# Pairs of weight chunks split by one instruction in the first layer's experts, and the router in column tiles

## The reference

```python
x = x + ga1 * out_l
h2_l = modulate(rmsnorm(x, g_norm2[i]), sh2, sc2)      # rmsnorm * (1 + scale) + shift
aff = sigmoid(h @ w_router); sel = aff + b_router      # 16 scores per token
# group of 4 experts by its best two; the two best experts in it; gates from aff
for e in range(16):
    he = silu(h @ w_e_gate[e]) * (h @ w_e_up[e])
    y = y + gates[:, e:e+1] * (he @ w_e_down[e])
```

## Time and profile before

| | us |
|---|---|
| median of three runs | 1566.52 |
| lowest, highest | 1563.4, 1567.39 |
| the profiled execution | 1565.73 |
| its span, first to last instruction | 1563.8 |

### The profile page before, as it was taken

How to read it: one execution, slowest core, us unless ns; L and a number is a source line. 1 busy time by engine, 2 the same in 40 slices (tenths; PEclk the granted TensorE clock), 3 DMA queues, 4 the chain that set the end, 5 groups by cost and what they waited for, 6 DMA issues and landing times.

```text
span 1563.8 us, 20838 instructions
## 1 busy us (share of the span) xinstructions
PE 1393.5 (89%) x7774; PEld 1019.3 (65%) x7774; DVE 791.1 (51%) x1268; ACT 674.7 (43%) x1098; POOL 166.8 (11%) x194
## 2 busy tenths in 40 slices
PE   5699999999998987999999955999989877998882
PEld 2478777885557855788888844998875865543330
DVE  1512344425775536999999937474358642000002
ACT  3442122334664224788888844542257530111002
POOL 4210110002320001021111120000000001111001
PEclk9699999999998996999999987999999987999997
DMA  8663564325862223899999962463230458999994
GB/s 297 240 221 131 189 242 148 95 95 189 257 201 95 95 81 119 304 380 383 383 380 376 365 230 87 143 221 108 95 135 1 149 202 321 414 416 415 414 415 160
DMA packets 117078, 359.35 MB, mean 230 GB/s; under 512 B 14570, under 2 KB 14891, under 8 KB 116355
## 3 DMA queue, kind: packets, MB, share of 16 engines
q1 hardware_dynamic: 91410, 272.86, 47.6%
q0 software_dynamic: 24720, 82.21, 15.0%
q10 hardware_dynamic: 864, 3.15, 0.5%
HBM read 345.57 MB, written 25.17 MB: 237 GB/s over the span
## 4 chain that ended last, share of the span: by engine, by line
PE 76%; DMA 13%; DVE 5%; ACT 3%; issue 2%; POOL 1%; POOLq 0%; SPq 0%; ACTq 0%; DVEq 0%
PE ps L545 18%; PE ps L547 18%; PE ps L546 18%; DMA ring<-in_w_e_gate 9%; PE ps L1085 3%; PE ps L797 3%; PE ps L911 2%; PE ps L888 2%; PE ps L815 2%; DMA w_raw<-in_w_ada 1%; PE ps L1107 1%; DMA ring<-in_w_e_down 1%; PE ps L1028 1%; PE ps L981 1%; PE ps L899 1%
## 5 line engine op out<-in xcount | busy, mean ns | idle before, releaser
L541 DVE TENSOR_TENSOR w_lo<-w_raw,w_hi 128x1024 fp32r<-128x1024 f32 x224 | 270.9, 1224 | 309.3 <-ACT w_hi L537 307.4
L537 ACT ACTIVATE w_hi<-w_raw 128x1024 fp32r<-128x1024 f32 x224 | 235.5, 1058 | 326.4 <-PE ps L547 324.5
L545 PE MATMUL ps<-h_hi,w_hi 128*128 128x512 f32 (+1 forms) x704 | 249.5, 354 | 14.8 <-DVE h_lo L1527 9.1
L546 PE MATMUL ps<-h_lo,w_hi 128*128 128x512 f32 (+1 forms) x704 | 246.9, 351 | 0.0
L547 PE MATMUL ps<-h_hi,w_lo 128*128 128x512 f32 (+1 forms) x704 | 246.9, 351 | 0.0
L545 PEld LDWEIGHTS ps<-h_hi,w_hi 128*128 128x128 f32 x704 | 133.9, 190 | 37.0 <-DVE h_lo L1527 9.9
L1085 PE MATMUL ps<-ring,xT 128*64 128x256 f32 x1024 | 131.2, 391 | 17.8 <-DMA ring<-in_w_e_up 10.8
L546 PEld LDWEIGHTS ps<-h_lo,w_hi 128*128 128x128 f32 x704 | 134.0, 190 | 18.6 <-issue 0.2
L547 PEld LDWEIGHTS ps<-h_hi,w_lo 128*128 128x128 f32 x704 | 133.9, 190 | 18.7
L1085 PEld LDWEIGHTS ps<-ring,xT 128*64 128x64 f32 x1024 | 68.8, 138 | 80.9 <-DMA ring<-in_w_e_up 25.7
L541 DVE TENSOR_TENSOR w_lo_more<-w_raw,w_hi_more 128x1024 fp32r<-128x1024 f32 x96 | 115.3, 1223 | 5.2
(11 more groups left out here) (258 smaller groups left out, 2366.0 us busy)
## 6 DMA issues: line engine op xcount, KB each, us to landing
w_raw<-in_w_ada POOLq DMA_DIRECT2D x96, 512.0 KB, 5.5
w_raw<-in_w_e_gate SPq DMA_DIRECT2D x64, 512.0 KB
w_raw<-in_w_e_up SPq DMA_DIRECT2D x64, 512.0 KB
w_raw<-in_w_e_down SPq DMA_DIRECT2D x64, 512.0 KB
ring<-in_w_e_gate SPq DMA_DIRECT2D x64, 512.0 KB, 15.6
ring<-in_w_e_up SPq DMA_DIRECT2D x64, 512.0 KB
ring<-in_w_e_down SPq DMA_DIRECT2D x64, 512.0 KB, 15.5
w_raw<-in_w_in SPq DMA_DIRECT2D x56, 512.0 KB
```

The source lines that it names most:

```text
L537: act.activation(whi(n), raw[:, slot(n), :, :], ACT.Copy).then_inc(hi_ready, 1)
L541: dve.tensor_tensor(wlo(n), raw[:, slot(n), :, :], whi(n).bitcast(F32), ALU.subtract).then_inc(lo_ready, 1)
L545: pe.matmul(acc, sh, mh, start=first, stop=False, skip_group_check=True)
L546: pe.matmul(acc, sh, ml, start=False, stop=False, skip_group_check=True)
```

## The change

1. In the first layer's experts `split_hi2` and `split_lo2` handle two neighbouring chunks in one instruction of 128x2048. Each waits for both transfers and for the later of the two ring places, and signals both when done. The small steps that stood after three of four chunks now stand after two.
2. The router no longer reads `h2T`. Scores are computed from `X` itself: weights `wrs` = router x scale, made once by DVE, times `X`; the shift's part is a sum of its own, 16 matmuls with one column (8 in the second layer). `token_sums` puts this and the sums of squares into four tiles of 32 columns of the TensorE array. DVE copies the 128x257 result, three transposes turn it token-major, and the root, reciprocal and multiplication are done on small tiles (`token_scores`). The reciprocals are spread back to 128x512 by four transposes and a copy. `xn` has four buffers.
3. The tokens are turned in order of halves, behind `route`'s inputs.
4. In the first layer only the first group's `pick` and `ids` stay ahead of the experts; the other three are done among the first two experts' work (`later_picks`, `later_ids` on DVE and TensorE, in PSUM bank 7). POOL waits for the last of them before its first store.

```diff
+            for t in tiles[i]:
                 add_tile((i, "h2", t, half), "act")
         add_tile((i, "rank"), "dve")
-        for g in range(4):
...
+    def hi_lo(n):
+        r, hi_, lo_ = n % (2 * SPL), (whi4, whi8), (wlo4, wlo8)
+        two = slice(r % SPL, r % SPL + 2)
+        return hi_[r // SPL][:, two, :, :], lo_[r // SPL][:, two, :, :]
+
+    def split_hi2(act, n, it=None, per=0):
+
+        for m in (n, n + 1):
+            act.wait_ge(raw_in[slot(m)], raw_value(m, it, per))
+        act.wait_ge(w_used, scaled(n + 1 - 2 * SPL + 1, it, per))
+        act.activation(hi_lo(n)[0], raw[:, slot(n):slot(n) + 2, :, :], ACT.Copy).then_inc(hi_ready, 2)
+
+    def split_lo2(dve, n, it=None, per=0):
+        dve.wait_ge(hi_ready, scaled(n + 2, it, per))
+        hi_, lo_ = hi_lo(n)
+        dve.tensor_tensor(lo_, raw[:, slot(n):slot(n) + 2, :, :], hi_.bitcast(F32), ALU.subtract).then_inc(lo_ready, 2)
...
-                wait_emptied(pool, (i, "ids", 3))
+                pool.wait_ge(ids_out, 3)
...
+        def token_sums(i, ks):
+
+            key, o = (i, "n2"), KT * norms[f"n2_{i}"]
+            acc = bank(key)
+            sides = [(0, 1), (1, 0)][i:]
+            if ks[0] == 0:
+                take_tile(pe, key)
+                pe.wait_ge(small_in, 32)
+                pe.wait_ge(mod_b, i + 1)
+                for k in range(KT):
+                    for g, st in sides:
+                        r0 = 64 + 32 * g
+                        pe.matmul(acc[r0:r0 + NE, SEQ:SEQ + 1], wr[:, k, :], mod[i][:, 24 + k, st:st + 1],
+                                  start=k == 0, stop=k == KT - 1, skip_group_check=True)
+            for k in ks:
+                pe.wait_ge(n_sq, o + k + 1)
+                for g, st in sides:
+                    tc = slice(g * SEQ, (g + 1) * SEQ)
+                    pe.matmul(acc[32 * g:32 * g + 32, 0:SEQ], ones[:, 0:32], sq[:, k % 2, tc],
+                              start=k == 0, stop=k == KT - 1, skip_group_check=True)
+                    r0 = 64 + 32 * g
+                    m = pe.matmul(acc[r0:r0 + NE, 0:SEQ], wrs[:, k, st, :], X[:, k, tc],
+                                  start=False, stop=k == KT - 1, skip_group_check=True)
                 m.then_inc(n_squ if k < KT - 1 else tile_done, 1)
...
-            norm_sum(f"n2_{i}", (i, "n2"), c0, range(4, KT))
-            pe.wait_ge(small_in, 32)
-            key = (i, "log")
+            token_sums(i, range(4, KT))
+            wait_emptied(pe, (i, "n2"))
+            key = (i, "tk")
             take_tile(pe, key)
-            for k in range(KT):
-                pe.wait_ge(n_hf, KT * (2 * i + 1) + k + 1)
-                m = pe.matmul(bank(key)[0:NE, c0:T], wr[:, k, :], h2T[:, k, c0:T], start=k == 0, stop=k == KT - 1)
+            for j, src in enumerate((sums[:, 0:P], sums[:, P:2 * P], spread(sums[:, SEQ:SEQ + 1], [P, P]))):
+                m = pe.transpose(bank(key)[:, j * P:(j + 1) * P], src, ident)
...
-            key = (i, "aff")
+            key = (i, "rb")
             take_tile(pe, key)
             for t in tiles[i]:
-                m = pe.transpose(bank(key)[:, NE * t:NE * t + NE], affT[0:NE, t * P:(t + 1) * P], ident[0:NE, 0:NE])
+                m = pe.transpose(bank(key)[:, t * P:(t + 1) * P], spread(rstd[:, t:t + 1], [P, P]), ident)
...
+            def turn_h2(half):
+                pe.wait_ge(n_hf, KT * norms[f"n2_{i}"] + 4 * half + 4)
+                for t in tiles[i]:
...
+            turn_h2(0)
+            turn_h2(1)
...
+            def later_ids(g):
+                if g >= 2:
+                    pe.wait_ge(ids_out, g - 1)
+                slot_ids(g, ps[:, 7, :]).then_inc(ids_done, 1)
...
                     into_hidden(nb + 8 * e, e, 0)
+                    later_ids(1 + 2 * e)
                     if e:
                         turn_hidden(0)
                     into_hidden(nb + 8 * e + 4, e, 1)
+                    if e == 0:
+                        later_ids(2)
...
-            norm_rms(f"n2_{i}", col0[i])
-            act.wait_ge(mod_b, 1)
+            t0, key = tiles[i][0], (i, "tk")
+            wait_tile(act, key)
+            act.activation(std4[:, t0:].rearrange("p (g j) -> p g j", j=2),
+                           bank(key)[:, 0:2 * P].rearrange("p (j g c) -> p g j c", j=2, c=32)[:, i:2, :, 0],
+                           ACT.Sqrt, bias=epst[:, 0:1], scale=1.0 / D).then_inc(n_std, 1)
+            warm(ACT.Sigmoid)
+            wait_emptied(act, key)
+            act.activation(aff[:, t0:, :], lg[:, t0:, :], ACT.Sigmoid).then_inc(aff_ready, 1)
+            act.wait_ge(mod_b, i + 1)
             norm_apply(f"n2_{i}", col0[i], lambda k, s: sc2[i][:, k, s:s + 1], lambda k, s: mod[i][:, 24 + k, s:s + 1], False)
...
-            key = (i, "log")
-            warm(ACT.Sigmoid)
-            wait_tile(act, key)
-            act.activation(affT[0:NE, col0[i]:T], bank(key)[0:NE, col0[i]:T], ACT.Sigmoid).then_inc(free_act, 1)
-            for t in tiles[i]:
-                for half in range(2):
+            for half in range(2):
...
-                    split_hi(act, n + ch, it, 24)
+                for ch in range(0, count, 2):
+                    split_hi2(act, n + ch, it, 24)
...
-                        splits(n + 8, 3, it)
+                        splits(n + 8, 2, it)
                         result(n + 4, 2 * it + j, j, it)
-                        splits(n + 11, 1, it)
...
+                    xn_, room = (xn[:, k % 2], 2) if split else (xn4[:, k % 4], 4)
+                    if k >= room:
+                        dve.wait_ge(n_hf, o + k - room + 1)
+                    dve.tensor_tensor(xn_[:, c0:T], X[:, k, c0:T], rinv[:, c0:T], ALU.mult).then_inc(n_xn, 1)
...
+                    dve.wait_ge(small_in, 32)
+                    for st in range(2):
+                        ins = dve.tensor_tensor(wrs[:, :, st, :], wr[:, :, :], spread(sc2[i][:, :, st:st + 1], [P, KT, NE]), ALU.mult)
+                    link(ins)
...
+            t0, c0 = tiles[i][0], col0[i]
+            key = (i, "n2")
+            wait_tile(dve, key)
+            dve.tensor_copy(sums[:, :], bank(key)[:, 0:SEQ + 1]).then_inc(free_dve, 1)
+            key = (i, "tk")
+            turned_ = bank(key)[:, 0:3 * P].rearrange("p (j g c) -> p g j c", j=3, c=32)[:, 2 + i:4, :, 0:NE]
+            by_tile = lambda t_: t_.rearrange("p (g j) e -> p g j e", j=2)
+            dve.wait_ge(n_std, i + 1)
+            link(dve.reciprocal(rstd[:, t0:], std4[:, t0:]))
+            link(dve.tensor_tensor(by_tile(lg[:, t0:, :]), turned_[:, :, 0:2, :],
+                                   by_tile(spread(rstd[:, t0:].unsqueeze(2), [P, 4 - t0, NE])), ALU.mult))
+            dve.tensor_tensor(by_tile(lg[:, t0:, :]), by_tile(lg[:, t0:, :]),
+                              spread(turned_[:, :, 2:3, :], [P, 2 - i, 2, NE]), ALU.add).then_inc(free_dve, 1)
+            key = (i, "rb")
+            wait_tile(dve, key)
+            dve.tensor_copy(rinv[:, c0:T], bank(key)[:, c0:T]).then_inc(free_dve, 1)
...
+            picks(0)
+            if i == 0:
+                slot_ids(0)
+                for ch in range(0, 4, 2):
+                    split_lo2(dve, exp0[i] + ch)
+                return
+            for g in range(4):
+                if g < 3:
+                    picks(g + 1)
+                slot_ids(g)
+
+        def later_picks(g):
+            iota = spread(cs(C_IOTA, P).unsqueeze(1).unsqueeze(1), [P, 4, 4, P])
+            ex = slice(4 * g, 4 * g + 4)
+            dve.tensor_tensor(pick[:, :, ex, :], spread(mrank[:, :, ex].unsqueeze(3), [P, 4, 4, P]), iota,
+                              ALU.is_equal).then_inc(picked, 1)
+
+        def later_ids(g):
+            dve.wait_ge(ids_done, g)
+            dve.tensor_scalar(ids[:, 4 * g:4 * g + 4], ps[:, 7, 0:8:2], float(FAR), None, ALU.add).then_inc(ids_out, 1)
...
+                splits(nb + 4, 2)
+                later_picks(1)
+                splits(nb + 6, 2)
                 places(i)
-                splits(nb + 7, 1)
+                later_ids(1)
+                later_picks(2)
                 splits(nb + 8, 4)
+                later_ids(2)
                 tokens_lo(1)
+                later_picks(3)
                 hidden(nb + 8, 0)
-                splits(nb + 12, 4)
+                splits(nb + 12, 2)
+                later_ids(3)
+                splits(nb + 14, 2)
...
-                        splits(n + 8, 3, it)
+                        splits(n + 8, 2, it)
                         result(n + 4, 2 * it + j, j, it)
-                        splits(n + 11, 1, it)
+                        splits(n + 10, 2, it)
```

More of the change, by code:

```diff
@@ L232, in build @@
     wr = small("wr", [P, KT, NE])
+    wrs = small("wrs", [P, KT, 2, NE])
+    std4 = small("std4", [P, 4])
+    rstd = small("rstd", [P, 4])
     brb = small("brb", [P, NE])
@@ L444, in build @@
                 add_tile((i, "yT", k), "dve")
-    finish = {key: plan[(key[0], "WO", 1, 3)] + 0.5 if key[1:] == ("n2",) else t for key, t in plan.items()}
```

(32 more changed lines are left out.)

62 lines of the change are left out of this document (28 added, 34 removed).

## The result

The changed kernel takes 1578.36 us (median of 8 runs, 1572.53 to 1579.65) against 1566.98 (8 runs, 1563.4 to 1569.13): a ratio of 1.0066, 95% interval 1.0049 to 1.0083. It is 11.4 us slower. The forecast was 1558.3 us, with a range up to 1566; the case that came is the rival to which the prediction gave 1 in 10, the pairs that starve the DMA engines.

What follows compares the result with a forecast made beforehand. TensorE was taken to bound the first layer's experts, DVE and DMA close behind, with the router path exposed between projection and experts. Terms -7.0 - 4.7 + 6.5 + 0.7 - 3.7 = -8.2 us gave 1558.3 from 1566.5, range 1553.5 to 1566.

Steps and rivals of the forecast that it cites:

- the pairs that starve the DMA engines: First layer's experts: later, doubled loads run queues dry, 1.0 us an expert, +14, 1572 us; chance 0.10.
- Part 4, the pairs: First layer's steady stage: splitting chunks in pairs costs 0.05 us an expert for 14 experts, 0.7 us later.
- The slots' own loop is load, ACT, DVE: Steady stage: reloading a weight slot takes 10.1 us against 12.0 in which TensorE uses eight chunks, so it fits.
- 3.9 spare: Steady stage: TensorE needs a pair 8.4 us later, splits end at 4.5, leaving 3.9 us of slack.
- Part 1, sums on the way: First layer's projection: shift matmuls and packed sums make the last sum end net 0.6 us later.
- the rival of nearly free columns: Router's one-column matmuls in both layers cost almost nothing: 3.9 us less, 1554.4 us; chance 0.18.
- the packed row: adaLN product's profile row, eight 32-column records in 0.64 us, used to price one-column records at 0.08 us each.
- The column tiles do run together: Router sums: a tile's eight records take 0.64 us; the rival said 1.7, some 7 us in all, 1565, chance 0.04.
- Part 2: First layer, from last sum to `sel`: the new router path brings `sel` 7.0 us earlier, 8.7 after the last sum.
- Part 3, groups moved: First layer's first experts: moving three groups of `ids` gains 4.7 us before the transposes and costs 6.5 later.
- the prediction's other bound: First layer's first gather: with the second layer's gather time of 7.37 us, moving groups gains only 2.4 us.
- Part 5: Second layer's router: one-column matmuls add 1.3 us, the shorter path brings `sel` 3.7 us earlier.

Runs made afterwards that it cites:

- e1: The changed kernel with every chunk of the first layer's experts split singly on ACT and DVE, router and moved groups kept; 1558.44 us, 0.9948 of before.
- e3: The changed kernel with pairs on ACT alone, DVE splitting chunk by chunk; 1567.87 us, 1.0011 of before.
- e4: The changed kernel with pairs on DVE alone, ACT splitting chunk by chunk; 1565.93 us, 0.9991 of before.
- e8: The changed kernel with single splits and all four groups of ids ahead of the experts again, leaving only the router; 1554.62 us, 0.9928 of before.
- e10: The same kernel as e8, measured again; 1557.94 us, 0.9942 of before.
- e11: The same kernel as e1, measured again; 1559.45 us, 0.9956 of before.
- e5: The changed kernel with `xg_hi`, the hidden product and `xg_lo` ahead of the second gate pair; 1572.07 us, 1.0023 of before.
- e6: The changed kernel with only the gate pair directly ahead of `xg_hi` and `xg_lo` split in singles; 1568.62 us, 1.0006 of before.
- e7: The changed kernel loading only half of each down-weight chunk in the steady loop, a sixth fewer bytes, for timing only; 1568.72 us, 1.0004 of before.
- e9: The change made in e5, with `he_hi` and `he_lo` also moved ahead of a pair; 1573.61 us, 1.0032 of before.
- e13: The kernel of e9 with down-weight loads in the steady loop cut to half, a sixth fewer bytes; 1559.88 us, one run.
- e2: The kernel before with pairs alone on both engines, router and groups as before; 1581.6 us, 1.0097 of before.

## Why the prediction was wrong

*What bounds the kernel.* Right: TensorE bound the stage, DVE and the DMA engines (99.4%) close behind. The prediction saw how little was spare and then priced an edit that takes from it at 0.7 us.

*Part 4, the pairs: the step that failed.* 0.05 us an expert were taken; e1 against the change shows 1.2, 16.7 us in all and 20 in the medians. Two sentences carried it. "The slots' own loop is load, ACT, DVE", 10.1 "against the 12.0 us": it took 5.5 us for a load, from a stage where DMA had idle time. Here the gate loads in the chain took 6.5 to 7.9, and DVE's list adds the small steps and other pairs to the loop; it came to 18.5 to 19.9 for twelve chunks, against 18.0 that TensorE needs. "3.9 spare", for TensorE's need of a pair, counted weights only. `xg_lo` stands in the same list with 2.2 to spare, and the prediction did not look at it. The rival had the mechanism and nearly the size: with a loaded transfer of 7.4 it gave 12.65 for eight chunks, 1.0 an expert, 1572; the period of 19.16 is 12.8 for eight. What it lacked is the small steps behind the pair. It was held unlikely since "ACT waits for TensorE, not for transfers, so some slack is there". That wait was 0.3 us long each time, and the edit put 2.0 to 3.4 us into the loop: the slack should have been set against that number.

*Part 1, sums on the way.* That the total agrees (+0.8 for +0.6) is luck, and its terms are not right. Of the 32 one-column records 26 took 0.48 us together, 0.018 each, not 0.08; the rival of nearly free columns was true. The Trainium skill ("TensorEngine Tiling (Array Packing)", Instruction Overhead) leads to an estimated 0.025 a record, which the trace bears out better than the packed row did. That makes it 2.0 us cheaper than priced, so that the last sum should end 1.4 earlier than before, not 0.6 later. Over all profiled executions it does end earlier: at 578.5 on average in the sixteen kernels with the new router, at 579.4 and 579.9 in the two with the old one. With a scatter of 5.6 us that is a hint and no more. The column tiles do run together: the eight records of a tile stood within 0.64 us (577.53 to 578.17), as forecast.

*Part 2.* `sel` comes 9.07 us after the last sum, 8.7 were forecast; in every run with the router 9.05 to 9.54.

*Part 3, groups moved.* The price held: 1.84 us a group on TensorE (1.75 forecast), the second expert's products 24.2 us after the first transposes in e1 and 25.0 in the change (24.4 forecast), and 6.85 in all with single splits (6.5). The gain was 2.3 in place of 4.7 since the gather took 7.6 us from its issue to the first transposes; the prediction's other bound, 7.37 and a gain of 2.4, is what came. With single splits it takes 5.5 and the gain is 4.4: the missing 2.1 are the pairs' too, DVE's alone, as e3 and e4 show below.

*Part 5.* `sel` 5.99 after the last sum instead of 10.76: -4.8, forecast -5.0.

Without the pairs the sum would have been -8.9; e1 measured 8.3 under before, with a trace 5.6 shorter (its profiled execution was its slowest). For the router alone it would have been -10.7; e8 and e10 measured 12.2 and 9.8 under before, with traces 13.5 and 10.5 shorter.

## What to carry to other kernels

Before making an instruction longer in a pipeline that has room for N pieces, write the loop of one slot out in full, load, each engine and everything that stands between in its list, with load times from the same stage under the same traffic, and set it against the time in which the consumer uses N pieces. Then do the same for the small steps that stand behind the longer instruction: their slack, here 2.2 us, is not that of the weights. Here the DMA engines were over 99% full and the engine that the coarser pass relieved was not the bound: what it saved was worth nothing, and four more slots gave back, in the steady stage, the whole 1.2 us an expert that it cost.

## What the runs showed of the hardware

GpSimd's issue of the first gather takes longer beside a longer pass of DVE. The passes, the issue and the transposes that wait for the gather, in e3 (DVE in single splits, the first from 601.21 to 602.43):

```profile
601.21 4.62 DVE L545 TENSOR_TENSOR w_lo<-w_raw,w_hi 128x1024 fp32r<-128x1024 f32 x4
...
602.20 1.17 POOL L714 DMA_INDIRECT xg<-hbuf,ids  x1 [131.46 <-DVE ids L1805]
...
607.58 1.95 PE L1085 MATMUL ps<-cst,xg 128*128 128x128 f32 x8 [6.49 <-DMA xg<-hbuf,ids]
```

And in e4 (DVE in pairs, ACT in singles; the first pair from 602.43 to 604.72):

```profile
602.43 4.49 DVE L562 TENSOR_TENSOR w_lo<-w_raw,w_hi 128x2048 fp32r<-128x2048 f32 x2
...
603.42 2.25 POOL L714 DMA_INDIRECT xg<-hbuf,ids  x1 [133.14 <-DVE ids L1805]
...
611.13 1.95 PE L1085 MATMUL ps<-cst,xg 128*128 128x128 f32 x8 [8.82 <-DMA xg<-hbuf,ids]
```

1.17 against 2.25 us of issue, 5.4 against 7.7 us to the transposes. In both the issue ends 0.94 to 0.95 us after the pass beside which it started. The kernels with three groups moved fall into these two classes by DVE's splits alone: 5.4 to 5.5 in e1, e3 and e11, 7.6 to 7.7 in the change, e4, e5, e6, e7, e9 and e13. The Trainium skill ("SBUF — State Buffer", SBUF: two separate sides) says that a DVE instruction with two inputs in SBUF holds a port pair that it shares with GpSimd, for its whole length, against a GpSimd instruction that reads SBUF. A split's `w_lo` has two such inputs, and the 1.08 us by which the issue is longer is what the pass is longer by (1.06). The trace agrees for the issue.

The later landing is another matter. In e2 the first issue starts beside a `pick` of 2.28 us and takes 2.24 too, and yet its data land 5.2 us after its start, as in the kernel before (5.1), against 7.3 in the change. So a longer issue alone doesn't delay the data; whether the second long pass or the weight loads that go out beside the gather do, no run here separates. In the steady stage the issues don't sort as cleanly: those of the gathers take 1.0 us on average in e3 and 1.9 to 2.2 in the other kernels with single splits on DVE, 1.9 to 2.3 with pairs.
